# The Fourier transform over tokens on sums and differences, and an earlier split of the gated branch

## The reference

```
q, k, v, g, f = split_proj(h @ w_in)                  # f: 512 tokens x 512 columns, 4 groups of 128
o = bidir_retention(rope(q), rope(k), v)              # 8 heads
ret_d  = (normalised(o) * silu(g)) @ w_ret_out        # "the gated branch": yr = normalised(o) * silu(g)
z      = fft2(f per group, over tokens and over the 128 columns, ortho).real
four_d = z @ w_four_out
gates  = sigmoid(h @ w_branch_gate + b)               # g_r and g_f, 1024 wide each
x = x + g1 * ((g_r * ret_d + g_f * four_d) @ w_out)
x = x + g2 * conv_ffn(...)                            # then the final norm
```

## Time and profile before

| | us |
|---|---|
| median of three runs | 1701.67 (1699.79 to 1703.91) |
| the profiled execution, its own time | 1700.52 |
| its span, first to last instruction | 1698.8 |
| TensorE busy | 1623.7 |
| VectorE busy | 877.0 |
| ScalarE busy | 772.6 |
| the Fourier stage's steps with token or feature products | about 1119 to 1181 |
| first product of `yr` | 1194.16 |

### The profile page before, as it was taken

One profiled execution on the slowest core, in us unless ns is written; L12 is line 12 of the kernel. 1 busy time (PEld: TensorE's weight loads), 2 busy tenths in 40 slices (PEclk: granted clock), 3 DMA queues, 4 the chain that ended last, 5 costly groups with the idle time before them and its releaser, 6 DMA issues.

```text
span 1698.8 us, 19917 instructions
## 1 busy us (share of the span) xinstructions
PE 1623.7 (96%) x7655; PEld 1283.5 (76%) x7655; DVE 877.0 (52%) x1026; ACT 772.6 (45%) x908; POOL 117.8 (7%) x93
## 2 busy tenths in 40 slices
PE   6999999999789899879999999999999999999998
PEld 5777777788677778667788887876787788888886
DVE  6434334445478789786524243311464665555564
ACT  5554445223378688565533234332223443343343
POOL 1101001000123223200100000000000000000000
PEclk9999999999889999989999999999999999999999
DMA  5457553324379999712421121311323233333222
GB/s 145 137 179 242 189 169 127 96 74 144 132 267 346 353 358 354 258 67 67 149 74 51 49 74 49 118 59 50 124 79 96 75 100 99 96 94 106 74 81 69
DMA packets 183426, 232.38 MB, mean 137 GB/s; under 512 B 13820, under 2 KB 154424, under 8 KB 180032
## 3 DMA queue, kind: packets, MB, share of 16 engines
q1 hardware_dynamic: 175647, 218.88, 39.1%
q0 software_dynamic: 7712, 12.60, 2.1%
HBM read 228.80 MB, written 18.37 MB: 145 GB/s over the span
## 4 chain that ended last, share of the span: by engine, by line
PE 85%; DVE 5%; ACT 4%; DMA 4%; issue 2%; POOL 0%; SPq 0%; POOLq 0%; ACTq 0%; DVEq 0%
PE psum L442 20%; PE psum L444 20%; PE psum L443 20%; DMA hg<-h_rows,at_row 2%; PE psum L1793 2%; PE psum L1794 2%; PE psum L1795 2%; PE psum L2552 2%; PE psum L742 1%; PE psum L1820 1%; PE psum L824 1%; PE psum L1769 1%; PE psum L1822 1%; PE psum L1821 1%; DMA y_rows<-y_sb,at_row 1%
## 5 line engine op out<-in xcount | busy, mean ns | idle before, releaser
L442 PE MATMUL psum<-h_hi,w_hi 128*128 128x512 f32 x1160 | 465.9, 402 | 8.9 <-DVE h_lo L528 3.2
L444 PE MATMUL psum<-h_hi,w_lo 128*128 128x512 f32 x1160 | 453.6, 391 | 0.0
L443 PE MATMUL psum<-h_lo,w_hi 128*128 128x512 f32 x1160 | 453.3, 391 | 0.0
L419 DVE TENSOR_TENSOR w_lo<-raw,w_hi 128x2048 fp32r<-128x2048 f32 (+2 forms) x99 | 223.6, 2259 | 223.5 <-ACT w_hi L415 223.5
L442 PEld LDWEIGHTS psum<-h_hi,w_hi 128*128 128x128 f32 x1160 | 218.5, 188 | 70.5 <-issue 15.4
L444 PEld LDWEIGHTS psum<-h_hi,w_lo 128*128 128x128 f32 x1160 | 218.4, 188 | 46.9
L443 PEld LDWEIGHTS psum<-h_lo,w_hi 128*128 128x128 f32 x1160 | 218.7, 189 | 46.3 <-issue 3.6
L415 ACT ACTIVATE w_hi<-raw 128x2048 fp32r<-128x2048 f32 (+2 forms) x100 | 187.9, 1879 | 76.5 <-PE psum L444 68.5
L472 ACT ACTIVATE sq<-x 128x512 f32<-128x512 f32 x56 | 35.3, 632 | 158.6 <-DVE x L1342 105.2
L1749 DVE TENSOR_TENSOR w_lo_more<-raw_more,w_hi_more 128x2048 fp32r<-128x2048 f32 x34 | 77.8, 2288 | 19.0 <-ACT w_hi_more L1742 18.7
L1749 DVE TENSOR_TENSOR w_lo<-raw,w_hi 128x2048 fp32r<-128x2048 f32 x34 | 77.7, 2286 | 15.9 <-ACT w_hi L1742 15.6
(11 more groups left out here) (387 smaller groups left out, 2605.0 us busy)
## 6 DMA issues: line engine op xcount, KB each, us to landing
raw<-in_w_up SPq DMA_DIRECT2D x67, 512.0 KB, 7.4
wm_raw<-in_w_mod SPq DMA_DIRECT2D x24, 1024.0 KB, 5.7
raw<-in_w_in SPq DMA_DIRECT2D x18, 1024.0 KB
raw<-in_w_in SPq DMA_DIRECT2D x33, 512.0 KB
raw_more<-in_w_down SPq DMA_DIRECT2D x24, 512.0 KB, 5.4
raw<-in_w_gate SPq DMA_DIRECT2D x23, 512.0 KB, 5.2
raw_more<-in_w_gate SPq DMA_DIRECT2D x22, 512.0 KB, 5.4
raw_more<-in_w_up SPq DMA_DIRECT2D x22, 512.0 KB, 7.6
```

The lines of the kernel that those rows point to most:

```text
L419: dve.tensor_tensor(w_lo[j][:, 0:tiles, :], raw[j][:, 0:tiles, :], w_hi[j][:, 0:tiles, :].bitcast(F32), ALU.subtract).then_inc(G["lo_ready ...
L442: pe.matmul(to, w_hi[j][:, tile, :], hi_k, start=(k == 0), stop=False)
L443: pe.matmul(to, w_hi[j][:, tile, :], lo_k, start=False, stop=False)
L444: return pe.matmul(to, w_lo[j][:, tile, :], hi_k, start=False, stop=last)
```

## The change

The 512-point sum over tokens is folded. With early tokens a (0 to 255) and late tokens b (256 to 511), even frequencies need only a + b and odd frequencies only a - b, each with 256 rows of the tables. VectorE forms a - b in the late half of `f_t` and then 2a - (a - b) = a + b in the early half, in place, before the transform over columns (`fold`, one per group, in steps 2 to 5). TensorE's `over_features` waits for it instead of for the copies. The table `dft_l` holds tokens 0 to 255 only, with the even frequencies in columns 0 to 255 and the odd ones in columns 256 to 511: half the size. `over_tokens` does, for each parity, 2 token tiles x 2 parts = 4 matmuls of 256 columns, instead of 8 of 512. The result lies in the PSUM bank by parity, and `z_hi` and `z_lo` read it interleaved (`in_order`), to be in order of frequency again.

The memory before `dft_l` that it gives up is a placeholder, `z_room`. Chunks 0 to 3 of `yr_hi` lie over it, so that their copy and subtraction (`gated_hi`, `gated_lo`) now stand in steps 8 to 11; chunks 4 to 7 are where they were.

```diff
-    a = 2 * np.pi * (np.outer(t, t) % T) / T
+    to = np.concatenate([t[0::2], t[1::2]])
+    a = 2 * np.pi * (np.outer(t[:T // 2], to) % T) / T
...
-            dft_l = sb("dft_l", [P, 2, NT, T])
+            z_room = sb("z_room", [P, NT * T])
+            dft_l = sb("dft_l", [P, 2, NT // 2, T])
...
+        def in_order(g):
+            return psum[:, 5 + g % 2, :].rearrange("p (o j) -> p j o", o=2)
...
                 if g == 0:
                     pe.wait_ge(Z["z_const"], 32)
-                    pe.wait_ge(Z["z_f"], 4)
                     pe.wait_ge(H["t_state"], 32)
                 else:
                     pe.wait_ge(Z["z_copied"], g)
+                pe.wait_ge(Z["z_fold"], 2 * g + 2)
...
-                for n in range(8):
-                    i, part = n // 2, n % 2
-                    done = pe.matmul(psum[:, 5 + g % 2, :], fd[:, g, i, part * P:(part + 1) * P],
-                                     dft_l[:, part, i, :], start=(n == 0), stop=(n == 7))
+                for odd in range(2):
+                    cols = slice(odd * 2 * P, odd * 2 * P + 2 * P)
+                    for n in range(4):
+                        i, part = n // 2, n % 2
+                        done = pe.matmul(psum[:, 5 + g % 2, cols], fd[:, g, 2 * odd + i, part * P:(part + 1) * P],
+                                         dft_l[:, part, i, cols], start=(n == 0), stop=(n == 3))
...
+            def gated_hi(c):
+                act.activation(yr_hi[:, c, :], yr[:, c, :], ACT.Copy).then_inc(Z["z_yhi"], 1)
...
-                    act.activation(z_hi[:, g, :], psum[:, 5 + g % 2, :], ACT.Copy).then_inc(Z["z_hi"], 1)
+                    act.activation(z_hi[:, g, :].rearrange("p (j o) -> p j o", o=2), in_order(g), ACT.Copy)\
+                       .then_inc(Z["z_hi"], 1)
+                if t >= 8:
+                    gated_hi(t - 8)
             four_gate(act, 7)
-            for c in range(KC):
-                act.activation(yr_hi[:, c, :], yr[:, c, :], ACT.Copy).then_inc(Z["z_yhi"], 1)
+            for c in range(4, KC):
+                gated_hi(c)
...
+            def gated_lo(c):
+                dve.wait_ge(Z["z_yhi"], c + 1)
+                dve.tensor_tensor(yr_lo[:, c, :], yr[:, c, :], yr_hi[:, c, :].bitcast(F32), ALU.subtract)\
+                   .then_inc(Z["z_ylo"], 1)
+
+            def fold(g):
+                early, late = f_t[:, g, 0:2 * P], f_t[:, g, 2 * P:4 * P]
+                dve.wait_ge(Z["z_f"], g + 1)
+                dve.tensor_tensor(late, early, late, ALU.subtract).then_inc(Z["z_fold"], 1)
+                dve.wait_ge(Z["z_fold"], 2 * g + 1)
+                dve.scalar_tensor_tensor(out=early, in0=early, scalar=2.0, in1=late, op0=ALU.mult, op1=ALU.subtract)\
+                   .then_inc(Z["z_fold"], 1)
...
                 if t < 6:
                     rest[t]()
+                if 2 <= t < 6:
+                    fold(t - 2)
                 if 7 <= t < 11:
                     g = t - 7
                     dve.wait_ge(Z["z_hi"], g + 1)
-                    dve.tensor_tensor(z_lo[:, g, :], psum[:, 5 + g % 2, :], z_hi[:, g, :].bitcast(F32), ALU.subtract)\
+                    dve.tensor_tensor(z_lo[:, g, :].rearrange("p (j o) -> p j o", o=2), in_order(g),
+                                      z_hi[:, g, :].bitcast(F32).rearrange("p (j o) -> p j o", o=2), ALU.subtract)\
                        .then_inc(Z["z_lo"], 1)
-            for c in range(KC):
-                dve.wait_ge(Z["z_yhi"], c + 1)
-                dve.tensor_tensor(yr_lo[:, c, :], yr[:, c, :], yr_hi[:, c, :].bitcast(F32), ALU.subtract)\
-                   .then_inc(Z["z_ylo"], 1)
+                if t >= 8:
+                    gated_lo(t - 8)
+            for c in range(4, KC):
+                gated_lo(c)
```

More of the change, by code:

```diff
@@ L2502, in ret_gpsimd @@
             pool.tensor_tensor(near[:, :, :], near[:, :, :], near_b[:, :, :], ALU.add).then_inc(H["t_tab"], 1)
-        Z = semaphores("z_const", "z_f", "z_gate", "z_d", "z_copied", "z_l", "z_hi", "z_lo", "z_yhi", "z_ylo", "z_ret",
+        Z = semaphores("z_const", "z_f", "z_fold", "z_gate", "z_d", "z_copied", "z_l", "z_hi", "z_lo", "z_yhi", "z_ylo", "z_ret",
                        "z_bank", "z_sum", "z_mhi", "z_mlo")
```

## The result

The changed kernel takes 1688.16 us (median of seven runs, 1681.02 to 1693.90), the kernel before 1703.91 us (seven runs, 1699.79 to 1710.36); the ratio is 0.990 with a 95% interval of 0.988 to 0.992. Forecast was 1686.8 us, in a range of 1684.0 to 1690.0, and faster with a chance of 0.96. It is faster, the time lies in the range, and the saving that was forecast, 14.9 us, is a ratio of 0.991.

The account below looks back on a forecast made before the run. TensorE's instruction spacing was taken as the bound (busy 72.65 of 72.70 us in the stage). Savings of 13.6 + 1.25 = 14.9 us from the profiled 1700.52 gave 1685.6, plus 1.15 for the runs' median: 1686.8 us, range 1684.0 to 1690.0.

Parts of the forecast that it names:

- The products: TensorE's four token steps: 16 instructions each, spaced 0.216 us instead of 0.429, so 3.46 us instead of 6.87; saves 13.6 us.
- Rival A: Token-step products don't halve: at three quarters of the price 1693.6 us, chance 0.04; at no halving 1700.4, chance 0.01.
- three quarters: Straight-line estimate from the skill's figures for token-step products: 98 ns at 256 columns against 131 at 512.
- The early split: Before the first yr product: four copies and subtractions moved earlier shrink TensorE's gap from 2.12 to 0.87 us, saving 1.25.
- the hop from the sigmoid's end: Delay before TensorE's first yr product, taken as 0.13 us from the end of yr_lo on VectorE to TensorE's start.
- Rival C: TensorE's gap before the first yr product stays, only 13.6 us saved: 1688.1 us, chance 0.08.
- The fold: Eight VectorE instructions before the Fourier stage, 0.42 and 0.48 us each, fit into VectorE's gaps and cost nothing.
- Uncovered it would be 3.6 us: Claimed cost of VectorE's fold, 0.9 us per group, if its work were not hidden in VectorE's gaps.
- The interleaved reads: z_hi and z_lo after each token step: strided PSUM reads keep their prices, 0.60 and 0.69 us, and cost nothing.
- Rival B: Interleaved PSUM reads hold TensorE in gate halves behind token steps: 1692.0 to 1727.8 us; chance 0.04, half of it slower.
- The slack of 9.0 us: How long the last z_hi on ScalarE may take, before the last sigmoid, until TensorE waits.
- The total: Whole kernel: 13.6 + 1.25 = 14.9 us saved, median forecast 1686.8 us.

Follow-up runs that it names:

- e1: Changed kernel without the early split: all eight yr_hi and yr_lo again after the last sigmoid; 1690.2 us, stage 111.2 us.
- e2: Changed kernel with token-step products of 512 columns again, on the halved table (so the result is not the transform); 1703.4 us, ratio 1.000 to the kernel before.
- e7: Changed kernel with the first yr slot done half by half, the first half not waiting for the last sigmoid; 1687.22 us.
- e4: Changed kernel with the fold moved from steps 2 to 5 to steps 5 to 8 of VectorE's program; 1710.79 us, ratio 1.005 to the kernel before.
- e3: Changed kernel with z_hi and z_lo reading PSUM contiguously, output tokens in another order; 1687.32 us.
- e5: Changed kernel with each z_hi copy done six times in sequence, 24 interleaved ScalarE reads instead of 4; 1687.4 us.
- e6: Changed kernel with only the last z_hi done 22 times in sequence, reads lasting 13.8 us; 1694.7 us.
- a0: The changed kernel itself, run again beside the others; 1695.58 us, ratio 0.992 to the kernel before.

## Why the prediction was right

**The products (13.6 us forecast, 13.6 and 13.7 measured in e1 and e2).** The step that carried it was to take the spacing of the neighbour of the same type and shape, 0.216 us, from the chain and not the mean duration of the rows; measured is 3.45/16 = 0.2156. Rival A, a price that does not halve, is out: 3.45/6.87 = 0.50. For f32 products of these sizes the estimate from the Trainium skill's "TensorE: Matmul & The Clock Gate", Back-to-back issue gap (three quarters), is not borne out after the change either.

**The early split (1.25 us forecast, 1.3 to 1.4 measured).** The gap is 0.78 us instead of the 0.87 forecast: the hop from the sigmoid's end (1181.86 + 0.69 = 1182.55) to TensorE (1182.60) is 0.05 us, shorter than the 0.13 that I took from VectorE's. Rival C, that the gap stays, did not happen. e7 shows that the rest of the gap hung on the sigmoid alone, as it is gone when the wait for it is. The first product behind a wait takes some 0.25 us extra, which the prediction did not have; it is there before and after (0.47 and 0.50 us), so it cancels in the forecast.

**The fold (nothing forecast, nothing measured).** The waits on `z_fold` never hold TensorE. The instructions took 0.42 and 0.42 us where I had 0.42 and 0.48. "Uncovered it would be 3.6 us" was the weak sentence of the prediction: e4 shows 22.1 us. Uncovered work doesn't cost its own length but the length of everything that is queued ahead of it when TensorE arrives (in two of the three waits a split on ScalarE, 1.9 us, and one on VectorE, 2.3 us, then the fold; in the first the end of the last retention head), and then the clock.

**The interleaved reads (nothing forecast, nothing measured).** Their lengths are those of plain reads, 0.60 and 0.69 us, and TensorE's spacing doesn't change under them, with 4 or with 24 reads (e3, e5). Rival B is out for this kernel. The prediction's picture of it was wrong in one point: it spoke of a bank next to the one that TensorE writes, where the reads are in bank 5 or 6 and the gate halves go to 0 and 1. The Trainium skill's rule in "Advanced Engine Details and Errata", Memory Cachelines, on non-contiguous patterns in PSUM, which slow matmuls, does not show for a strided reader of such a bank. The slack of 9.0 us that I had worked out was 9.4 (e6).

**The total (1686.8 forecast, 1688.2 measured).** The stage gained 15.0 us where 14.9 were forecast. Between the medians it is 15.8 us (1703.91 - 1688.16). The forecast started from a median of three runs, 1701.67 us, and seven runs of the same kernel gave 1703.91; from there it would have been 1689.0. So the 1.4 us between forecast and median are a base 2.2 us too low, less 0.9 us by which the medians differ more than forecast. Neither is the change's, by the stage: the profiled execution reached the stage 3.5 us later than the one before did, and a0 7.2 us later still, with the same code up to there. The range was wide enough for this median, but not for the second one of the same kernel, 1695.58 us: it allowed 1.5 us for a median, read off three runs, where medians of six or seven runs differ by 7. That the first median fell inside was partly luck.

## What to carry to other kernels

Where TensorE is busy without a gap, the price of halving a product's columns is the difference of two spacings in the chain, and a neighbour of the same type and shape gives it exactly. Work that is put on another engine for it is free only while its cover holds, and the way to price the lack of cover is to add up what stands ahead of it on that engine at the moment TensorE needs it: 0.85 us of fold, asked for late, cost 7 to 8 us in each of three groups and nothing in the fourth. When runs spread more than the effect, cut the span at events that both kernels have: the stage repeated to 0.1 us while the time of the same kernel moved by 7.

## What the runs showed of the hardware

A wait of TensorE of 5.1 to 5.3 us cost 1.7 to 2.9 us more than its length (e4, e6), as the work right behind it runs at a granted clock of 0.5 to 0.6; waits of 0.8 and 2.1 us, with the clock at 1.00 behind them, cost about 0.25 us more than their length (first product 0.50 and 0.47 us in the chain, then 0.23; with the wait of 0.8 gone e7 gained 1.0). The Trainium skill has this in "TensorE: Matmul & The Clock Gate", "HAM oscillation — how this bites in real kernels": a matmul stream that waits long enough for the clock to drop starts its next stretch at the low level. The trace agrees.

A TensorE without a gap in the records can be at either level of the clock. In the routing, in narrow f32 instructions, a0 shows it busy for 10.00 of 10.00 us at a clock of 0.52: it had been without a gap since 438.0 us when the clock fell between 440 and 442. In e3 the same eight chunks, behind the same wait of 0.8 us, ran at 1.00 to their end. From the routing's first transpose to the experts' part that was 31.1 us in e3 and 40.9 in a0. What decides between the two is open.

Interleaved reads of f32 from PSUM, neighbours 256 elements apart, take ScalarE and VectorE as long as contiguous ones (598 against 597 ns on ScalarE, 691 against 692 on VectorE). Gate halves into bank 0 or 1 kept their 5.47 us while bank 5 or 6 was read so (5.48 in e5).
